# The last unit of expert weights in transfers of 8 partitions for rows 0 to 63 and one transfer of 64 rows for the rest

## What is computed

```
logits = h @ router_w                          # 256 tokens x 16 experts
affinity = softmax(logits)
gate, idx = top_k(affinity.T, 32)              # each expert takes 32 tokens
xe = h[idx]                                    # 16 x 32 x 1024
hidden = silu(xe @ w_gate[e]) * (xe @ w_up[e]) # 32 x 2048 per expert
ye = (hidden @ w_down[e]) * gate               # 32 x 1024 per expert
out = x + scatter_add(idx, ye)
```

## Time and profile before

| | us |
|---|---|
| median of 3 runs | 1834.52 (1833.77 to 1836.62) |
| span of the profiled execution | 1833.6 |
| TensorE busy, matmuls / weight loads | 1452.6 / 948.1 |
| VectorE busy | 690.4 |
| ScalarE busy | 526.4 |
| GpSimd busy | 120.2 |
| DMA: moved over the span, mean rate | 542 MB, 296 GB/s |

### The profile page before, as it was taken

How to read it: one execution, slowest core, us unless ns; L and a number is a source line. 1 busy time by engine, 2 the same in 40 slices (tenths; PEclk the granted TensorE clock), 3 DMA queues, 4 the chain that set the end, 5 groups by cost and what they waited for, 6 DMA issues and landing times.

```text
span 1833.6 us, 24308 instructions
## 1 busy us (share of the span) xinstructions
PE 1452.6 (79%) x10234; PEld 948.1 (52%) x10243; DVE 690.4 (38%) x1171; ACT 526.4 (29%) x877; POOL 120.2 (7%) x147
## 2 busy tenths in 40 slices
PE   7999999999999999999896556656565565665555
PEld 7887888887888889988642112111122111211111
DVE  5676666666666667887620000000000000000000
ACT  6545443654444576566510000000000000000000
POOL 0151000012000011042200000000000000000000
PEclk9999999999999999999997787787877777778777
DMA  9533555543455544424789999999999999999997
GB/s 268 184 122 130 187 188 184 177 144 116 162 193 194 192 142 138 137 97 184 317 354 428 427 428 427 427 428 427 427 429 427 427 428 427 428 428 428 427 427 318
DMA packets 139139, 542.02 MB, mean 296 GB/s; under 512 B 10157, under 2 KB 103554, under 8 KB 114466
## 3 DMA queue, kind: packets, MB, share of 16 engines
q1 hardware_dynamic: 138824, 540.46, 74.7%
q0 software_dynamic: 48, 0.13, 0.0%
q10 hardware_dynamic: 170, 0.04, 0.0%
HBM read 539.56 MB, written 1.05 MB: 295 GB/s over the span
## 4 chain that ended last, share of the span: by engine, by line
PE 46%; DMA 45%; DVE 5%; ACT 2%; issue 1%; POOL 0%; ACTq 0%; DVEq 0%; SPq 0%; POOLq 0%
DMA ew<-in_expert_w_gate_dram 15%; DMA ew<-in_expert_w_up_dram 15%; DMA ew<-in_expert_w_down_dram 14%; PE bank L1301 8%; PE bank L1608 7%; PE bank L1302 7%; PE bank L1303 7%; PE bank L1606 4%; PE bank L1986 3%; DVE wHL L2040 1%; PE bank L2017 1%; PE bank L1605 1%; PE bank L1524 1%; ACT wHL L819 1%; PE bank L1322 1%
## 5 line engine op out<-in xcount | busy, mean ns | idle before, releaser
L1986 PE MATMUL bank<-ew,xeT 128*32 128x512 f32 x2048 | 338.7, 796 | 226.3 <-DMA ew<-in_expert_w_up_dram 123.7
L2040 DVE TENSOR_TENSOR wHL<-ring,wHL 128x2048 fp32r<-128x2048 f32 (+1 forms) x124 | 284.3, 2294 | 103.6 <-ACT wHL L819 103.0
L1986 PEld LDWEIGHTS bank<-ew,xeT 128*32 128x32 f32 x2048 | 64.6, 129 | 483.9 <-DMA ew<-in_expert_w_up_dram 206.3
L819 ACT ACTIVATE wHL<-ring 128x2048 fp32r<-128x2048 f32 (+1 forms) x124 | 236.6, 1908 | 244.9 <-PE bank L1608 132.1
L2017 PE MATMUL bank<-ew,tok 128*32 128x256 f32 x2048 | 174.4, 500 | 103.8 <-DMA ew<-in_expert_w_down_dram 97.7
L1608 PE MATMUL bank<-xHL,wHL 128*128 128x512 f32 x588 | 209.9, 396 | 0.0
L2745 DVE TENSOR_TENSOR tok<-tok,bank 128x512 f32<-128x512 f32 x16 | 11.0, 687 | 512.9 <-PE bank L1986 512.9
L2017 PEld LDWEIGHTS bank<-ew,tok 128*32 128x32 f32 x2048 | 77.1, 137 | 194.0 <-DMA ew<-in_expert_w_down_dram 117.8
L1606 PE MATMUL bank<-xHL,wHL 128*128 128x256 f32 x672 | 174.1, 279 | 0.0
L2749 DVE TENSOR_TENSOR h<-h,bank 128x512 f32<-128x512 f32 x64 | 39.7, 682 | 322.3 <-PE bank L2025 322.3
L1606 PEld LDWEIGHTS bank<-xHL,wHL 128*128 128x128 f32 x672 | 126.6, 188 | 8.2
(11 more groups left out here) (354 smaller groups left out, 2243.7 us busy)
## 6 DMA issues: line engine op xcount, KB each, us to landing
ew<-in_expert_w_gate_dram SPq DMA_DIRECT2D x64, 2048.0 KB, 46.0
ew<-in_expert_w_up_dram SPq DMA_DIRECT2D x64, 2048.0 KB, 45.8
ew<-in_expert_w_down_dram SPq DMA_DIRECT2D x62, 2048.0 KB, 46.3
ring<-in_w_gate_up_dram SPq DMA_DIRECT2D x44, 1024.0 KB, 5.0
ring<-in_w_down_dram SPq DMA_DIRECT2D x22, 1024.0 KB, 4.8
ring<-in_w_in_dram SPq DMA_DIRECT2D x22, 1024.0 KB, 5.2
ring<-in_w_out_dram SPq DMA_DIRECT2D x12, 1024.0 KB, 4.9
ring<-in_w_in_fox_dram SPq DMA_DIRECT2D x10, 1024.0 KB, 9.8
```

Source lines behind the costliest of these rows:

```text
L819: act.activation(split_part(n, 0, 0, w.stop), ring[:, slot(n), w], ACT.Copy).then_inc(w_hi, 1)
L1986: mm = pe.matmul(bank[half][32 * j:32 * j + 32, :], xeT[:, k, CAP * e:CAP * e + CAP], w_[:, m, 512 * j:512 * j + 512], start=(k == 0), sto ...
L2040: op = dve.tensor_tensor(split_part(n, 1, c0, c1 - c0), ring[:, slot(n), c0:c1], split_part(n, 0, c0, c1 - c0).bitcast(F32), ALU.subtract)
```

## The change

For the last unit, each half of its columns is no longer one transfer of 128 rows but nine transfers: rows 0 to 63 in eight transfers of 8 rows, then rows 64 to 127 in one of 64 rows. The small transfers of the first half count on `x_in[0]`, those of the second on `x_in[1]`, on top of the 16 that each holds; the 64 rows of the first half count on `mem_in[0]`, those of the second on `e_rest`. TensorE waits for the small ones and the large one of each half before the matmuls that need them. Bytes, places in `ew`, the matmuls and their order stay.

```
+        NEAR = 64
...
+        e_near, e_far = x_in, mem_in[0]
...
                 for part in range(2):
                     c = slice(EW // 2 * part, EW // 2 * part + EW // 2)
-                    sp.dma_start(ew[:, eslot(g), c], src[:, c]).then_inc((e_full[eslot(g)], e_rest)[part], 16)
+                    for r in range(0, NEAR, 8):
+                        sp.dma_start(ew[r:r + 8, eslot(g), c], src[r:r + 8, c]).then_inc(e_near[part], 16)
+                    sp.dma_start(ew[NEAR:P, eslot(g), c], src[NEAR:P, c]).then_inc((e_far, e_rest)[part], 16)
...
                 for j in range(4):
-                    w_ = arrived(8 + j).rearrange("p (m d) -> p m d", m=4)
+                    if e * EU + 8 + j == LAST:
+                        pe.wait_ge(e_near[0], 16 + 16 * (NEAR // 8))
+                        pe.wait_ge(e_far, 16 + 16)
+                        w_ = ew[:, eslot(LAST), :].rearrange("p (m d) -> p m d", m=4)
+                    else:
+                        w_ = arrived(8 + j).rearrange("p (m d) -> p m d", m=4)
                     for m in range(4):
                         if e * EU + 8 + j == LAST and m == 2:
+                            pe.wait_ge(e_near[1], 16 + 16 * (NEAR // 8))
                             pe.wait_ge(e_rest, 16)
```

## The result

The changed kernel takes 1842.73 us (median of 5 runs, 1841.36 to 1846.75), the kernel before 1834.52 beside it (5 runs, 1833.75 to 1836.62). The ratio is 1.0049 with a 95% interval of 1.0038 to 1.0060. It is slower by about half a per cent, and lies above the prediction of 1834.9 and its range to 1840.2.

A forecast was written before the change was run, and what follows sets the result against it. The prediction took the gapless stream of expert weights as the bound, the change acting only on the last landing. Terms summed to +0.4 us (+0.35 sharing, +0.05 waits): 1834.9 us, range 1833.2 to 1840.2.

The forecast's parts named there:

- term 7: Last unit's DMA: eight engines writing eight neighbouring partitions at once; between nothing and +10.1 us on the landing, taken as +0.35.
- the eight engines are the early ones: Kernel tail: 8-row transfers run on the eight engines through by about 1817.7, idle 4 to 7 us; forecast's chance 0.45.
- term 1: DMA of the last unit: late engines relieved by 2.45 us, so the second half lands at 1822.72 instead of 1825.17.
- its sign that TensorE waits over 3 us ahead of its last 16 matmuls: Kernel end: such a wait would show rivals 1 and 3; 0.6 to 2.5 us was the forecast's.
- Rival 3: Last unit: late engines among the eight and shared paths, +4.9 to +7.3 us, taken +5.5, 1840.0; chance 0.17.
- Rival 1: Last unit: neighbouring partitions share one path at full price, early engines favoured; +4.5 to 5 us, 1839.0; chance 0.10.
- Rival 2: Last unit: the eight are the late engines or hold the latest of them; +2.45 us, 1837.0; chance 0.25.
- Rival 4: SP's queue: each issue takes 3.46 us, the last at 1842.0, some 17 us late; chance 0.03.
- Term 4: TensorE before the last unit's matmuls: three more waits, 0 to 0.1 us, taken as 0.05.
- term 2: TensorE at the last unit: with weights there it goes on at 1824.64, so the gain is capped at 0.58 us.
- The 0.95 us around the span: Outside the profiled span: some 0.95 us between the span of 1833.6 and the median of 1834.52.
- The upper end of the sum: Whole kernel: the summed effect of +0.4 us was put between -0.5 and +2.2 us.

The follow-up runs named there:

- count24: Against near_only_spread, eight more spread 8-row transfers into a free slot, so the eight engines carry 24 pieces; last half landed at 1825.13.
- spread: Against the changed kernel, each 8-row transfer takes rows four apart, in DRAM and tile alike; 1839.85 us, ratio to before 1.0031.
- two64: Against the changed kernel, rows 0 to 63 of each half go in one transfer of 64 rows instead of eight small ones; landing at 1832.28.
- far_only: Against the changed kernel, only the two transfers of rows 64 to 127 of the last unit, rows 0 to 63 left out; landing at 1829.50.
- near_only: Against the changed kernel, the two transfers of 64 rows left out, only the 8-row transfers of neighbouring rows remain; landing at 1826.20.
- near_only_spread: Against the changed kernel, the 64-row transfers left out and the rows of each 8-row transfer taken four apart; landing at 1822.61.
- cols8: Against the changed kernel, each half in eight transfers of all 128 rows by 1 KB; 1836.28 us against 1836.16 for before.
- probe: Kernel before with loads of 16 KB rows in various row patterns added behind its output, with nothing beside them; its time is not compared.

## Why the prediction was wrong

**What failed: term 7, and the premise under it.** The prediction knew that eight engines writing eight neighbouring rows at once was in no row, bounded it by 0 and +10.1 us on the landing, and took +0.35, "because it is nearest to the row of today's landing". It measures +5.93. Two things in that step were wrong, and the experiments split them (last landings of one profiled execution each; in brackets the same counted from each one's first piece, which takes out where its stream stood):

```
before                                            1825.17  (14.24)
24 pieces on the eight engines, nothing shared    1825.13  (14.30)   count24    0.0  (+0.1)
+ transfers of 64 rows                            1828.76  (18.01)   spread    +3.6  (+3.7)
+ neighbouring rows in the small transfers        1831.10  (20.67)   after     +2.3  (+2.7)
```

First, the term looked at the small transfers alone. The transfer of 64 rows was counted as "four rows each" and priced at nothing; it costs +3.6 here, +7.1 on the landing when it comes twice (two64), and +4.3 alone (far_only), with 6.7 us on the unit before the last. Which part is the larger depends on the order in which they are added, since both hold up the same engines: without the transfers of 64 rows, the neighbouring rows alone cost 3.6 us, or 5.4 from the first piece (near_only against near_only_spread), and not +2.3. The last unit of before ran at full rate not because 16 engines can write anywhere at 26.75 GB/s, which is how the lower bound was read out of the earlier trace rows, but because every transfer in that window spans 128 rows; two64 divides the same rows in two and halves the rate. The row was right and did not carry the conclusion. The Trainium skill (DMA: Bandwidth & Descriptors, section The descriptor swizzle) has each engine of a 128-row transfer write the rows of one port, its own; cols8, with rows of 16 KB at 0.632 us, agrees in the rate, and no record shows which engine writes which row. Second, the term's staggering, "neighbours in time overlap for a third", was too mild: with nothing but neighbours (near_only) the 128 pieces took 0.441 us in the mean where 0.310 is the time undisturbed (near_only_spread), 2.1 us more for 16 of them, and in the kernel after all 256 took 0.521, 1.7 times 0.306.

**The premise "the eight engines are the early ones".** Six are and two are not. Taken alone the count is worth nothing: the landing 1822.72 of term 1 was not to be had, since the two late ones come to 1825.13. What the prediction takes from the Trainium skill beside it (DMA: Bandwidth & Descriptors, section Why a DMA increments its semaphore by 16 and not by 1), that such a transfer takes the lowest-numbered engines, can't be tested, as no record numbers engines; what is shown is that they aren't the eight early ones.

**What was not in any term.** The early engines don't only delay themselves. Rows of 16 KB of the units before take 1.064 us instead of 0.628 as soon as the early engines are in the last unit, and so the unit before the last lands 5.0 us late. The prediction had it as given that this unit arrives at 1820.27. For the same reason its sign that TensorE waits over 3 us ahead of its last 16 matmuls misled: it waits 1.56 us there, because it waited 5.24 us one step earlier. Its other signs of shared paths were there: pieces over 0.31 us (0.521), and a rate per active engine under 26.75 GB/s (205 over 16 engines at a share of 0.96 is 13.3). Nothing before 1810 changed: the fall begins with the last unit.

**The rivals.** Rival 3 (0.17) comes nearest: one late engine among the eight is enough, and paths are shared; it gave +5.5 and 1840.0 for a landing that moved by 5.93. Its working, 24 pieces on the last engine at 1.5 to 2 times their time, is not where the time went: 5.0 of the 5.9 us are there already when the unit before the last lands, so most of it was lost before the last pieces. Rival 1 has the mechanism and the wrong engines. Rival 2, the count alone at +2.45, is refuted by count24: the relieved engine was the latest. Rival 4 is refuted by SP's rows.

**What held.** The tail behind the landing is unchanged but for 0.1 us (8.5 against 8.4). Term 4 has it within its range: 0.14 us lie between the landing and the matmuls where there were 0.04, though the change adds two waits and not the three that the term names. SP's issues took 0.3 to 1.8 us each, 18 were through at 1798.1 and hidden, a little later than the 1790.5 to 1796 worked out. Small transfers run on eight engines: the page counts 139267 packets against 139139, 128 more, which is 16 transfers with eight completions and two with 16, less two with 16. TensorE's cap, term 2, held where the landing was early enough: near_only_spread does its 64 matmuls in one go. The clock of its matmuls stayed where it was: the 48 took 4.40 us against 4.33, the last 16 1.07 in both. The 0.95 us around the span were misread: they are 1.8, and the profiled execution lies 0.9 above the median. The forecast was made on the median and is not moved by that. The upper end of the sum, +2.2, isn't what its own latest landing gives (1826.8 less 1825.17 is 1.6, with the waits 1.7); the outcome lies beyond either.

**Why the median moved by more than the landing.** Five runs of after lie 5.4 us apart, five of before 2.9. How much is lost may depend on when the engines meet, which could differ between executions; this was not tested.

## What to carry to other kernels

A transfer should span all 128 rows, also the last one: dividing it by rows moves work between engines and at the same time puts several engines on one path into the on-chip memory, which costs more (+3.6 and +2.3 us here) than evening them out could give. If it must be divided, dividing by columns cost 0.9 us on the landing for 16 parts, but its issues took SP 41 us, so the queue has to be that far ahead. Rows 4 apart kept full speed for rows 0 to 63 with nothing else in the last unit; all 128 rows divided so were not run. And a window of full rate speaks for the pattern of rows that was in it and for no other; look at GB/s beside the share, because in these runs a shared path left the share near 1.

## What the runs showed of the hardware

- Neighbouring rows of the on-chip memory share a path for DMA writes: 64 rows in a block 5.4 us, every second row 3.7 us; eight transfers of 8 neighbours at once 15.2 us, of rows 4 apart 7.1; one transfer of 8 neighbours lands 3.82 us after its issue, of rows 4 apart 2.26.
- An engine held up on such a path counts as busy: 188 GB/s at a share of 1.00, where 446 goes with 1.06.
- The holding up reaches transfers of 128 rows that are under way: 0.63 us a row of 16 KB became 1.06. Part of it may be rows of these units on the same path, but in near_only, where only half the rows are in dispute, 84 of 100 such rows took 0.68 us or more, against 3 of 93 in the kernel before. How it reaches them wasn't settled.
- The DMA engines drift apart in a stream of 900 us (in the kernel before their shares of unit 190 land between 1811.4 and 1813.0 for eight and between 1817.3 and 1820.3 for the others), and the eight that small transfers use hold six of the early and two of the late ones. What holds the late ones back was not tested.
- A small transfer of rows 4 apart takes SP longer to issue: eight in 5.32 us against 2.64 for neighbours, in the probe.
